# FFN products of the unnormed input, with mean, deviation and bias put in behind them

## The chip, the cores and the metric

The kernel runs on one core of one Trainium2 chip. The metric is the device time of one execution in microseconds (us), as a median of several runs. The engines that matter are PE (TensorE, the matrix unit), DVE (VectorE), ACT (ScalarE), POOL (GpSimd) and SP (SyncE, which here only issues DMAs).

## The reference

One step of a two-layer decoder trunk: layer 0 mixes tokens with RWKV-7, layer 1 with a causal pooling mixer; behind each stands a SwiGLU FFN, and behind every sublayer a layer norm. There are 288 token columns (256 of a prompt, 32 of samples), D = 2048 and a hidden width of 5632, all in fp32.

```python
def _layer_norm(x, g, b):
    mu = jnp.mean(xf, axis=-1, keepdims=True)
    var = jnp.mean(jnp.square(xf - mu), axis=-1, keepdims=True)
    return ((xf - mu) * lax.rsqrt(var + LN_EPS) * g + b)
...
x = _layer_norm(ALPHA * x + mixer(x), ln_g, ln_b)
x = _layer_norm(ALPHA * x + (silu(x @ w_gate) * (x @ w_up)) @ w_down, ln_g, ln_b)
```

## The kernel before

**Layout.** Activations lie transposed: 128 channels on the partitions, 16 chunks of channels (KC), T = 288 token columns in a row. `X` holds the residual, `MH`/`ML` the input of a product, split into a high part in fp32r and the rest.

**One product.** An fp32 product is three fp32r matmuls of 128 x 128 weights with 288 columns (`three`, L723 to L725: high by high, low by high, high by low). Weights come in slabs of 128 x 2048 values for 16 such products. SP issues the DMA of a slab into one of four raw buffers `RAW`; ACT copies its high part to `WH` (`hi`, L1247); DVE subtracts it from the raw one to get `WL` (`lo`, L1677); PE then does the slab's 48 matmuls into one PSUM bank. `WH` and `WL` have two slots, so `hi` of a slab waits until PE has ended the slab two before it. Every engine works through its own instructions in the order in which they are written.

**Start.** The 16 chunks of x are transposed on PE and copied out by ACT and DVE in a loop over c, which also forms r's mixed input (`mix_hi` L1256, `mix_lo` L1692). `first_hi` and `first_lo` put the first two slabs of r between the steps c of that loop. PE waits for all banks of x to be free, then does r's two first columns, alternately by halves of k, then column 2 (`RH`, `RL`), and so on.

**FFN.** Each of the two FFNs has 88 up slabs, alternately of gate and of up, then the down slabs. For a pair of slabs ACT takes the sigmoid of the gate bank (L1552), DVE multiplies it by the gate and the up bank (L2174, L2177), ACT copies the high part `HH` (L1554) and DVE takes the rest `HL` (L2182). In the code of both engines this chain stands behind the `hi` or `lo` of a slab and ahead of the next one's.

**Layer norm ahead of an FFN** (L1522 to L1534 on ACT, L2076 to L2092 on DVE, L1087 and L1094 on PE; norm 0 ahead of FFN 0, norm 2 ahead of FFN 1). A matmul with a constant matrix gives the mean in a bank; DVE centres X in place, four chunks at a time; ACT squares; PE sums the squares over 12 rows (DVE adds the last four rows to the four ahead of them); ACT takes the root and DVE its reciprocal. Then, chunk by chunk, DVE scales by gain and reciprocal, ACT adds the bias once into `MH` and once into X, DVE takes `ML`; PE starts slabs 0 and 1, k by k alternately, as these arrive. A third slab lies split in `W3H`/`W3L`. What stands ahead of norm 0 are the "late" units of the attention's output projection, whose banks DVE adds to X (L2046); ahead of norm 2 it is the pooling mixer (L2295).

```python
for k in range(KC):
    pe.wait_ge(ln["lo"], HALVED[lnk] + k + 1)
    first = up(0, k)
    second = up(1, k)
```

Of the kernel before, what the change touches and what calls it, by code (L numbers as in the profile page):

```python
# [132 lines left out]
def build(nc, x_prompt, x_sample, state_wkv, state_shift, state_pool, ln_g, ln_b, rw_mu, rw_wr, rw_wk, rw_wv,  # L133
# [4 lines left out]
    with ctx:  # L138
# [33 lines left out]
        ML[0] = at("ML0", [P, KC, T], F32R, after("MH0"))  # L172
# [16 lines left out]
        OP = at("OP", [P, KC, T], F32, place["MH1"][0])  # L189

# [158 lines left out]
        hl_ready = sem("hl_ready")  # L349
        act_self = sem("act_self")  # L350
# [121 lines left out]
        ln = {n: sem("ln_" + n) for n in ("x", "mean", "cen", "sq", "var", "sd", "rstd", "scaled", "done", "lo", "sum", "pairs")}  # L472
# [247 lines left out]
        def _(pe):  # L720
# [33 lines left out]
            def first(n, k):  # L754
# [327 lines left out]
            def layer_norm(k):  # L1082
                if k == 2:
                    mean_of(range(13, KC))
                else:
                    pe.wait_ge(ln["x"], KC)
                    pe.matmul(PS[4][:, 0:T], AVG, SUM[:, :], start=True, stop=True).then_inc(ln["mean"], 1)  # L1087
                for q in range(3):
# [29 lines left out]
            def ffn(layer, lnk):  # L1118
                for g in range(2):
# [1239 lines left out]
```

## Time and profile before

| what | us |
|---|---|
| time, median of 3 runs | 2698.59 (2695.88 to 2700.09) |
| time of the profiled execution | 2697.64 |
| span in its trace | 2696.1 |
| PE busy | 2575.9 (96%) |
| DVE busy | 1578.6 (59%) |
| ACT busy | 1131.6 (42%) |
| POOL busy | 142.6 (5%) |

The span runs from the first to the last instruction in the trace; the profiled execution's time has 1.5 us around it. Busy time on PE is that of matmuls which overlap, so it is not PE at its best. In the page's chain of work that ended last, followed back from the end, 82% of the span lie on PE. The DMA engines are busy about half of the time.

### The profile page before, as it was taken

The page shows a single profiled execution, that of the slowest core. Times are in us where ns is not written, and L with a number is a line of the kernel's source. Part 1 is how long each engine was busy: PE and PEld are TensorE (multiplying, and loading weights), DVE is VectorE, ACT ScalarE, POOL GpSimd, SP SyncE. Part 2 cuts the span into 40 slices and gives each one's busy share as a digit, 9 for nine tenths or more (in the row PEclk, how much of TensorE's full clock was granted, in tenths as well). Part 3 has the DMA queues.
Part 4 walks back from the last instruction along what each step waited for, and adds up shares of the span by engine and source line. Part 5 has one row for each costly group of instructions (what it writes and reads, how often), then busy time and mean ns, then how long its engine had stood idle before and what let it go on. Part 6 is the DMA issues. An engine that isn't in the chain of part 4 may idle for free.

```text
span 2696.1 us, 56356 instructions
## 1 busy us (share of the span) xinstructions
PE 2575.9 (96%) x23305; PEld 2476.5 (92%) x23305; DVE 1578.6 (59%) x2400; ACT 1131.6 (42%) x1596; POOL 142.6 (5%) x211
## 2 busy tenths in 40 slices
PE   7989999999999899999999999969999999999997
PEld 7978888888789899999999999958999999999997
DVE  7877888888856644444444444686444444444446
ACT  5565555555533533333333333445333333333334
POOL 0000111111101000000000000100000000000000
PEclk9989999999999899999999999979999999999999
DMA  7622223322336656555665556624555566565553
GB/s 198 197 77 73 80 80 84 84 83 82 92 91 196 156 163 171 160 145 163 187 171 161 165 143 167 175 69 125 166 161 166 145 167 190 160 170 163 142 167 94
DMA packets 707051, 379.33 MB, mean 141 GB/s; under 512 B 16023, under 2 KB 699191, under 8 KB 706711
## 3 DMA queue, kind: packets, MB, share of 16 engines
q1 hardware_dynamic: 701040, 363.46, 48.4%
q0 software_dynamic: 5792, 13.34, 1.9%
q8 instruction: 114, 1.87, 0.3%
q10 hardware_dynamic: 70, 0.39, 0.1%
q14 instruction: 35, 0.29, 0.0%
HBM read 367.31 MB, written 10.62 MB: 140 GB/s over the span
## 4 chain that ended last, share of the span: by engine, by line
PE 82%; DVE 11%; ACT 4%; issue 2%; DMA 1%; POOL 0%; DVEq 0%; ACTq 0%; SPq 0%; POOLq 0%
PE PS L723 25%; PE PS L724 24%; PE PS L725 24%; PE PS L874 2%; DVE WL L1677 2%; ACT WH L1247 1%; DVE PL L1794 1%; DVE ML L1692 1%; PE PS L906 1%; DVE TM L1685 1%; DMA PR<-in_rw_wk 1%; PE PS L993 0%; PE PS L948 0%; PE PS L911 0%; DVE XL L1933 0%
## 5 line engine op out<-in xcount | busy, mean ns | idle before, releaser
L1677 DVE TENSOR_TENSOR WL<-RAW,WH 128x2048 fp32r<-128x2048 f32 (+1 forms) x325 | 658.8, 2027 | 765.6 <-ACT WH L1247 765.6
L723 PE MATMUL PS<-MH,WH 128*128 128x288 f32 (+1 forms) x3152 | 931.2, 295 | 27.0 <-DVE ML L2092 11.3
L724 PE MATMUL PS<-ML,WH 128*128 128x288 f32 (+1 forms) x3152 | 933.7, 296 | 0.0
L725 PE MATMUL PS<-MH,WL 128*128 128x288 f32 (+1 forms) x3152 | 932.7, 296 | 0.0
L1247 ACT ACTIVATE WH<-RAW 128x2048 fp32r<-128x2048 f32 (+1 forms) x325 | 553.6, 1704 | 823.0 <-PE PS L725 808.5
L723 PEld LDWEIGHTS PS<-MH,WH 128*128 128x128 f32 (+1 forms) x3152 | 595.7, 189 | 31.5 <-issue 13.3
L724 PEld LDWEIGHTS PS<-ML,WH 128*128 128x128 f32 (+1 forms) x3152 | 595.7, 189 | 0.2
L725 PEld LDWEIGHTS PS<-MH,WL 128*128 128x128 f32 (+1 forms) x3152 | 595.0, 189 | 0.0
L724 PE MATMUL PS<-HL,WH 128*128 128x288 f32 x1408 | 415.3, 295 | 0.0
L725 PE MATMUL PS<-HH,WL 128*128 128x288 f32 x1408 | 415.0, 295 | 0.0
L723 PE MATMUL PS<-HH,WH 128*128 128x288 f32 x1408 | 413.4, 294 | 0.0
L723 PEld LDWEIGHTS PS<-HH,WH 128*128 128x128 f32 x1408 | 264.7, 188 | 0.1
L724 PEld LDWEIGHTS PS<-HL,WH 128*128 128x128 f32 x1408 | 264.7, 188 | 0.1
L725 PEld LDWEIGHTS PS<-HH,WL 128*128 128x128 f32 x1408 | 264.5, 188 | 0.0
L723 PE MATMUL PS<-MH,PH 128*128 128x288 f32 x768 | 245.0, 319 | 8.4 <-DVE ML L2022 3.8
L724 PE MATMUL PS<-ML,PH 128*128 128x288 f32 x768 | 229.4, 299 | 0.0
L725 PE MATMUL PS<-MH,PL 128*128 128x288 f32 x768 | 228.4, 297 | 0.0
L723 PEld LDWEIGHTS PS<-MH,PH 128*128 128x128 f32 x768 | 146.9, 191 | 33.5 <-issue 22.4
L1554 ACT ACTIVATE HH<-TM 128x288 f32 (+1 forms) x88 | 39.2, 445 | 258.7 <-DVE TM L2177 258.7
L724 PEld LDWEIGHTS PS<-ML,PH 128*128 128x128 f32 x768 | 147.2, 192 | 0.3
L725 PEld LDWEIGHTS PS<-MH,PL 128*128 128x128 f32 x768 | 147.0, 191 | 0.0
L1794 DVE TENSOR_TENSOR PL<-PR,PH 128x512 fp32r<-128x512 f32 x144 | 92.5, 653 | 49.8 <-ACT PH L1348 48.7
(313 smaller groups left out, 2725.1 us busy)
## 6 DMA issues: line engine op xcount, KB each, us to landing
RAW<-in_ffn_w_in SPq DMA_DIRECT2D x176, 1024.0 KB, 5.7
RAW<-in_ffn_w_down SPq DMA_DIRECT2D x128, 704.0 KB, 4.8
RAW<-in_rw_wr SPq DMA_DIRECT2D x16, 1024.0 KB, 6.1
PR<-in_rw_wk SPq DMA_DIRECT2D x64, 256.0 KB, 3.2
PR<-in_rw_wv SPq DMA_DIRECT2D x64, 256.0 KB, 3.1
PR<-in_rw_wo SPq DMA_DIRECT2D x64, 256.0 KB, 3.4
S0N<-in_state_wkv POOLq DMA_DIRECT2D x64, 64.0 KB, 2.3
out<-SOS POOLq DMA_DIRECT2D x64, 64.0 KB, 2.8
```

What stands on the lines that cost most here:

```text
L723: pe.matmul(out, wh, xh, start=first, stop=False)
L724: pe.matmul(out, wh, xl, start=False, stop=False)
L725: return pe.matmul(out, wl, xh, start=False, stop=last)
L874: ins = pe.matmul(bank[hr[r], col + u * CH:col + (u + 1) * CH], lhs(hr[r], u), rhs(hr[r], u), start=True, stop=True)
L906: pe.transpose((PA, PB)[t][:, n * P:(n + 1) * P], f[:, t * P:(t + 1) * P], IDN)
L1247: act.activation(WH[0:rows, j % 2, 0:n], RAW[0:rows, j, 0:n], ACT.Copy).then_inc(hi_ready, 1)
L1554: act.activation(HH[:, bass.ds(hc, 1), :].rearrange("p a t -> p (a t)"), TM[:, b, :], ACT.Copy).then_inc(hh_ready, 1)
L1677: dve.tensor_tensor(WL[0:rows, j % 2, 0:n], RAW[0:rows, j, 0:n], WH[0:rows, j % 2, 0:n].bitcast(F32), ALU.subtract).then_inc(lo_ready, 1)
L1685: dve.scalar_tensor_tensor(out=TM[:, c % 2, :], in0=XX[:, c, :], scalar=PAR[:, row:row + 1], in1=X[:, c, 1:T + 1], op0=ALU.mult, op1=ALU.a ...
L1692: dve.tensor_tensor(ML[m][:, c, :], mixed, MH[m][:, c, :].bitcast(F32), ALU.subtract)\
L1794: dve.tensor_tensor(PL[slot][0:rows, 0:n], PR[slot][0:rows, 0:n], PH[slot][0:rows, 0:n].bitcast(F32), ALU.subtract).then_inc(pc_lo, 1)
```

## The change

The normed input of an FFN is (h - mean) * rstd * g + b. A product with it is rstd * (W (g h) - mean * (W g)) + W b. The changed kernel takes W (g h) with `UH`/`UL`, which hold g h of the unnormed h and behind its 288 columns two more, g and b; so each up matmul has 290 columns, and the bank of a slab gets W g and W b in its columns 288 and 289. The rows of `UH`/`UL` are 1160 bytes long where those of `MH`/`ML` are 1152.

- `UH` (ACT, `input_hi`) and `UL` (DVE, `input_lo`) are formed chunk by chunk in the loop of late units and in the pooling mixer.
- PE does slab 0 whole, with the mean's matmul behind its twelfth k, then slab 1, then the variance (`ln_var`), then the third slab.
- The chain of a pair: ACT copies the two columns of both banks to `C12`; DVE subtracts mean by W g from each bank, multiplies each by rstd; ACT takes the sigmoid with W b as bias; DVE adds W b to the gate and multiplies, the same for the other half; then `HH` and `HL`. That is 7 DVE and 4 ACT instructions where there were 3 and 2.
- The normed X itself, which the residual needs, is formed later: `scaled` (DVE) and `normed` (ACT), a loop of 16 each behind the chain of slabs 2 and 3.
- `lo` of FFN 0's slab 0 stands in the late loop behind the add of unit 12, that of slab 1 behind the loop; both stood behind the norm's centring; `third_lo` stands between centring and the sum of the last four rows.
- r's column 0 goes to bank 6, PE doesn't wait for all of x's banks ahead of it, and the two first slabs are split earlier (`first_hi` behind c = 6 and 11 where it was 10 and 15, `first_lo` behind 8 and 12 where it was 12 and 18).

```diff
+        UH = at("UH", [P, KC, T + 2], F32R, place["MH0"][0] - 128)
+        UL = at("UL", [P, KC, T + 2], F32R, place["ML0"][0] - 128)
...
+        NLN = at("NLN", [P, 2, T], F32, place["LHH"][0] + 4 * T)
+        C12 = at("C12", [P, 2, 4], F32, after("NLN"))
+        GATE = at("GATE", [P, 2, T], F32, after("C12"))
+        LIN = at("LIN", [P, 2, T], F32, after("GATE"))
...
+        def first_bank(n):
+
+            return n % 4 if n else 6
...
-                return three(PS[n % 4][0:wd, 0:T], wh, wl, MH[m][:, k, :], ML[m][:, k, :], k == 0, k == KC - 1)
-
-            pe.wait_ge(x_bank_free, 6 + KC)
+                return three(PS[first_bank(n)][0:wd, 0:T], wh, wl, MH[m][:, k, :], ML[m][:, k, :], k == 0, k == KC - 1)
...
+                if n == 1:
+                    pe.wait_ge(x_bank_free, 6 + KC - 2)
...
+            pe.wait_ge(x_bank_free, 6 + KC)
...
-                        return three(PS[j][:, 0:T], WH[:, j % 2, k * P:(k + 1) * P], WL[:, j % 2, k * P:(k + 1) * P],
-                                     MH[0][:, k, :], ML[0][:, k, :], k == 0, k == KC - 1)
+                        return three(PS[j][:, 0:T + 2], WH[:, j % 2, k * P:(k + 1) * P], WL[:, j % 2, k * P:(k + 1) * P],
+                                     UH[:, k, :], UL[:, k, :], k == 0, k == KC - 1)
...
-                        take_slab(s0 + 1)
-                        take_bank(o0 + 1)
-                        for k in range(KC):
-                            pe.wait_ge(ln["lo"], HALVED[lnk] + k + 1)
-                            first = up(0, k)
-                            second = up(1, k)
-                        first.then_inc(slab_used, 1)
-                        second.then_inc(slab_used, 1)
+                        for j in range(2):
+                            take_slab(s0 + j)
+                            take_bank(o0 + j)
+                            for k in range(KC):
+                                if j == 0:
+                                    pe.wait_ge(ln["lo"], HALVED[lnk] + k + 1)
+                                ins = up(j, k)
+                                if j == 0 and k == KC - 5:
+                                    ln_mean(lnk)
+                            ins.then_inc(slab_used, 1)
+                        ln_var(lnk)
                         third_slab()
...
-                if c in (10, 15):
-                    first_hi(0 if c == 10 else 1)
+                if c in (6, 11):
+                    first_hi(0 if c == 6 else 1)
...
+            def input_hi(k, c):
+
+                act.wait_ge(out_free, 4 + OUT["o" if k == 0 else "pool"] + (c if c < 12 else KC - 1) + 1)
+                act.activation(UH[:, c, 0:T], X[:, c, 1:T + 1], ACT.Copy, scale=par("ln_g", k * KC + c))\
+                   .then_inc(ln["hi"], 1)
...
+            def normed(k):
+
                 with act.Fori(0, KC) as c:
                     act.wait_ge(ln["scaled"], k // 2 * KC + c + 1)
                     xc = X[:, bass.ds(c, 1), 1:T + 1].rearrange("p a t -> p (a t)")
-                    act.activation(MH[0][:, bass.ds(c, 1), :].rearrange("p a t -> p (a t)"), xc, ACT.Identity,
-                                   bias=par("ln_b", k * KC + c))
                     act.activation(xc, xc, ACT.Identity, bias=par("ln_b", k * KC + c)).then_inc(ln["done"], 1)
...
-                                act.activation(TM[:, b, :], PS[j - 1][:, 0:T], ACT.Sigmoid).then_inc(sg_ready, 1)
+                                act.activation(C12[:, b, 0:2], PS[j - 1][:, T:T + 2], ACT.Copy)
+                                act.activation(C12[:, b, 2:4], PS[j][:, T:T + 2], ACT.Copy).then_inc(sums_out, 1)
+                                act.wait_ge(gate_scaled, n + 1)
+                                act.activation(GATE[:, b, :], TM[:, b, :], ACT.Sigmoid, bias=C12[:, b, 1:2])\
+                                   .then_inc(sg_ready, 1)
                                 act.wait_ge(hid_ready, n + 1)
-                                act.activation(HH[:, bass.ds(hc, 1), :].rearrange("p a t -> p (a t)"), TM[:, b, :],
+                                act.activation(HH[:, bass.ds(hc, 1), :].rearrange("p a t -> p (a t)"), LIN[:, b, :],
                                                ACT.Copy).then_inc(hh_ready, 1)
                     if g == 0:
                         up(0, False)
+                        normed(2 * layer)
...
-                if c in (12, 18):
-                    first_lo(0 if c == 12 else 1)
+                if c in (8, 12):
+                    first_lo(0 if c == 8 else 1)
...
+            def input_lo(k, c):
+                dve.wait_ge(ln["hi"], HALVED[k] + c + 1)
+                dve.scalar_tensor_tensor(out=UL[:, c, 0:T], in0=X[:, c, 1:T + 1], scalar=par("ln_g", k * KC + c),
+                                         in1=UH[:, c, 0:T].bitcast(F32), op0=ALU.mult, op1=ALU.subtract)\
+                   .then_inc(ln["lo"], 1)
...
+                            if m == 12:
+                                lo(SLAB["ffn0"], 0)
+                            if 1 <= m <= 12:
+                                dve.wait_ge(ln["hi"], m)
+                                if m == 1:
+                                    gains_lo(0, 0, 12)
...
+            lo(SLAB["ffn0"] + 1, 1)
...
-            def layer_norm(k, beside):
+            def layer_norm(k):
                 n = k // 2
                 dve.wait_ge(ln["mean"], n + 1)
+                dve.wait_ge(ln["lo"], HALVED[k] + KC)
+                dve.tensor_scalar(NLN[:, 0, :], PS[4][:, 0:T], -1.0, None, ALU.mult)
                 for q in range(4):
                     xs = X[:, 4 * q:4 * q + 4, 1:T + 1]
                     dve.tensor_tensor(xs, xs, PS[4][:, 0:T].unsqueeze(1).broadcast_to([P, 4, T]), ALU.subtract)\
                        .then_inc(ln["cen"], 1)
+                third_lo(SLAB["ffn0"] if k == 0 else SLAB["ffn1"])
                 dve.wait_ge(ln["sq"], 4 * n + 4)
                 dve.tensor_tensor(SQ[:, 8:12, :], SQ[:, 8:12, :], SQ[:, 12:16, :], ALU.add).then_inc(ln["pairs"], 1)
-                beside()
                 dve.wait_ge(ln["sd"], 2 * n + 2)
-                dve.reciprocal(LNS[:, 1, :], LNS[:, 0, :]).then_inc(ln["rstd"], 1)
+                dve.reciprocal(NLN[:, 1, :], LNS[:, 0, :]).then_inc(ln["rstd"], 1)
                 dve.wait_ge(ln["rstd"], n + 1)
                 dve.wait_ge(ln["cen"], 4 * n + 4)
 
-                def scaled(c):
+            def scaled(k):
+                with dve.Fori(0, KC) as c:
                     dve.scalar_tensor_tensor(out=xcur(c), in0=xcur(c), scalar=par("ln_g", k * KC + c),
-                                             in1=LNS[:, 1, :], op0=ALU.mult, op1=ALU.mult).then_inc(ln["scaled"], 1)
-                def low(c):
-                    dve.wait_ge(ln["done"], n * KC + c + 1)
-                    dve.tensor_tensor(one(ML[0], c), xcur(c), one(MH[0], c).bitcast(F32), ALU.subtract)\
-                       .then_inc(ln["lo"], 1)
-                for c in range(3):
-                    scaled(c)
-                with dve.Fori(0, KC - 3) as c:
-                    scaled(c + 3)
-                    low(c)
-                for c in range(KC - 3, KC):
-                    low(c)
-                third_lo(SLAB["ffn0"] if k == 0 else SLAB["ffn1"])
+                                             in1=NLN[:, 1, :], op0=ALU.mult, op1=ALU.mult).then_inc(ln["scaled"], 1)
...
+                                gate, lin = TM[:, b, :], LIN[:, b, :]
+                                dve.wait_ge(sums_out, n + 1)
+                                dve.scalar_tensor_tensor(out=gate, in0=NLN[:, 0, :], scalar=C12[:, b, 0:1],
+                                                         in1=PS[j - 1][:, 0:T], op0=ALU.mult, op1=ALU.add)\
+                                   .then_inc(gate_lin, 1)
+                                dve.scalar_tensor_tensor(out=lin, in0=NLN[:, 0, :], scalar=C12[:, b, 2:3],
+                                                         in1=PS[j][:, 0:T], op0=ALU.mult, op1=ALU.add)\
+                                   .then_inc(lin_out, 1)
+                                dve.wait_ge(gate_lin, n + 1)
+                                dve.tensor_tensor(gate, gate, NLN[:, 1, :], ALU.mult).then_inc(gate_scaled, 1)
+                                dve.wait_ge(lin_out, n + 1)
+                                dve.sem_inc(out_free, 2)
+                                dve.tensor_tensor(lin, lin, NLN[:, 1, :], ALU.mult).then_inc(lin_scaled, 1)
                                 dve.wait_ge(sg_ready, n + 1)
-                                dve.tensor_tensor(TM[:, b, :], TM[:, b, :], PS[j - 1][:, 0:T], ALU.mult)\
-                                   .then_inc(hid_self, 1)
-                                dve.wait_ge(hid_self, n + 1)
-                                dve.tensor_tensor(TM[:, b, :], TM[:, b, :], PS[j][:, 0:T], ALU.mult)\
-                                   .then_inc(hid_ready, 1)
-                                dve.wait_ge(hid_ready, n + 1)
-                                dve.sem_inc(out_free, 2)
+                                dve.scalar_tensor_tensor(out=gate, in0=gate, scalar=C12[:, b, 1:2], in1=GATE[:, b, :],
+                                                         op0=ALU.add, op1=ALU.mult).then_inc(gated, 1)
+                                dve.wait_ge(lin_scaled, n + 1)
+                                dve.wait_ge(gated, n + 1)
+                                dve.scalar_tensor_tensor(out=lin, in0=lin, scalar=C12[:, b, 3:4], in1=gate,
+                                                         op0=ALU.add, op1=ALU.mult).then_inc(hid_ready, 1)
                                 dve.wait_ge(hh_ready, n + 1)
-                                dve.tensor_tensor(one(HL, hc), TM[:, b, :], one(HH, hc).bitcast(F32), ALU.subtract)\
+                                dve.tensor_tensor(one(HL, hc), lin, one(HH, hc).bitcast(F32), ALU.subtract)\
                                    .then_inc(hl_ready, 1)
 
                     if g == 0:
                         up(0, False)
+                        scaled(2 * layer)
```

On ACT, at the start of FFN 0, the loop over 16 chunks (L1529 to L1534) stands before ahead of the first `hi` of the loop of slabs:

```order
L1514 ACTIVATE W3H<-RAW 128x2048
L1526 ACTIVATE LNS<-PS 128x288
L1528 ACTIVATE LNS<-LNS 128x288
L1529 UNCONDITIONAL_BRANCH
L1529 ISA
L1532 ISA x2
L1532 ACTIVATE MH_60<-X,PAR 128x288
L1534 ACTIVATE X<-X,PAR 128x288
L1529 REGISTER_ALU
L1529 COMPARE_AND_BRANCH
L1247 ACTIVATE WH<-RAW 128x2048
L1552 ACT_TABLE_LOAD
```

And of the changed kernel, the same engine from the `hi` of slabs 4 and 5 (L1270) to that of slab 6 (the last row):

```order
L1270 ACTIVATE WH<-RAW 128x2048 x2
L1596 ACTIVATE C_88<-PS 128x2
L1597 ACTIVATE C_88<-PS 128x2
L1599 ACTIVATE GATE<-TM,C_88 128x288
L1602 ACTIVATE HH<-LIN 128x288
L1575 UNCONDITIONAL_BRANCH
L1575 ISA
L1578 ISA
L1578 REGISTER_ALU
L1578 ACTIVATE X<-X,PAR 128x288
L1575 REGISTER_ALU
L1575 COMPARE_AND_BRANCH
```

The loop of 16 (L1575 to L1578) has moved from ahead of the first slabs to a place behind the chain of slabs 2 and 3; it has one ACTIVATE in it where there were two, and the `hi` of slab 6 stands right behind it.

On PE, between the last late unit (`PL`) and the first products of the FFN (`WH`), before:

```order
L725 MATMUL PS<-MH_60,PL_83 128x288
L1087 MATMUL PS<-SUM,CP 128x288
L1094 MATMUL PS<-SQ,CP 128x288 x12
L723 MATMUL PS<-MH_60,WH 128x288
L724 MATMUL PS<-ML_61,WH 128x288
```

And after, behind the products of slab 1 (`WL` in the first row), at the third slab (`W3H`):

```order
L742 MATMUL PS<-UL,WH 128x290
L743 MATMUL PS<-UH,WL 128x290
L1116 MATMUL PS<-SQ,CP 128x288 x12
L741 MATMUL PS<-UH,W3H 128x290
L742 MATMUL PS<-UL,W3H 128x290
```

The twelve sums of squares have moved from ahead of slab 0 to behind slab 1, and the products read rows of 290 columns.

## Rows read from the trace of the kernel before

**Rows 1.** The page: busy time by engine, and the chain by engine.

```profile
PE 2575.9 (96%) x23305; PEld 2476.5 (92%) x23305; DVE 1578.6 (59%) x2400; ACT 1131.6 (42%) x1596; POOL 142.6 (5%) x211
...
PE 82%; DVE 11%; ACT 4%; issue 2%; DMA 1%; POOL 0%; DVEq 0%; ACTq 0%; SPq 0%; POOLq 0%
```

**Rows 2.** Stretches: us, PE busy (count), granted clock, DMA share, GB/s.

```profile
950.00:1150.00 200.00, 200.00 (x1515) 1.00 0.60 165
...
902.00:917.00 15.00, 15.00 (x99) 0.87 0.13 34
```

**Rows 3.** Timeline of PE at norm 0: start, us, what, idle before.

```profile
882.70 0.29 PE L725 MATMUL PS<-MH,PL 128*128 128x288 f32 x1
...
892.58 3.56 PE L1094 MATMUL PS<-SQ,CP 128*128 128x288 f32 x14
...
901.88 0.58 PE L723 MATMUL PS<-MH,WH 128*128 128x288 f32 x1 [5.74 <-DVE ML L2092]
902.25 0.44 PE L724 MATMUL PS<-ML,WH 128*128 128x288 f32 x1
902.49 0.44 PE L725 MATMUL PS<-MH,WL 128*128 128x288 f32 x1
...
916.54 0.40 PE L723 MATMUL PS<-MH,W3H 128*128 128x288 f32 x1
```

**Rows 4.** Timeline of PE at the start, r's columns 0 and 2.

```profile
28.69 0.61 PE L723 MATMUL PS<-MH,WH 128*128 128x288 f32 x1 [10.24 <-DVE XPS L1704]
...
43.05 0.29 PE L723 MATMUL PS<-MH,RH 128*128 128x288 f32 x1
```

**Rows 5.** Timeline of DVE at the start: `lo` of r's first two slabs.

```profile
23.84 2.28 DVE L1677 TENSOR_TENSOR WL<-RAW,WH 128x2048 fp32r<-128x2048 f32 x1
...
30.59 2.28 DVE L1677 TENSOR_TENSOR WL<-RAW,WH 128x2048 fp32r<-128x2048 f32 x1
```

**Rows 6.** Timelines of DVE and ACT at norm 0.

```profile
885.20 5.15 DVE L2076 TENSOR_TENSOR X<-X,PS 128x1152 f32<-128x1152 f32 x4 [1.71 <-PE PS L1087]
891.58 1.36 DVE L2079 TENSOR_TENSOR SQ<-SQ 128x1152 f32<-128x1152 f32 x1 [1.23 <-ACT SQ L1522]
...
897.26 1.95 DVE L2082 RECIPROCAL LNS<-LNS 128x288 f32<-128x288 f32 x1
899.24 1.81 DVE L2087 SCALAR_TENSOR_TENSOR X<-X,PAR,LNS 128x288 f32<-128x288 f32 x4
...
918.66 1.28 ACT L1552 ACT_TABLE_LOAD   x1
```

**Rows 7.** Timeline of PE at norm 2: last means, first product, third slab.

```profile
1811.30 2.45 PE L1202 MATMUL PS<-X,CP 128*128 128x288 f32 x8
...
1829.89 0.58 PE L723 MATMUL PS<-MH,WH 128*128 128x288 f32 x1 [5.56 <-DVE ML L2092]
...
1844.72 0.29 PE L723 MATMUL PS<-MH,W3H 128*128 128x288 f32 x1
```

**Rows 8.** A pair of up slabs amid FFN 0: timelines of ACT and DVE.

```profile
1005.75 1.92 ACT L1247 ACTIVATE WH<-RAW 128x2048 fp32r<-128x2048 f32 x1 [4.43 <-PE PS L725]
...
1010.97 0.45 ACT L1554 ACTIVATE HH<-TM 128x288 f32 x1 [3.01 <-DVE TM L2177]
1012.10 1.92 ACT L1247 ACTIVATE WH<-RAW 128x2048 fp32r<-128x2048 f32 x1 [0.68 <-PE PS L725]
...
1009.91 0.45 DVE L2174 TENSOR_TENSOR TM<-TM,PS 128x288 f32<-128x288 f32 x1
...
1014.05 2.29 DVE L1677 TENSOR_TENSOR WL<-RAW,WH 128x2048 fp32r<-128x2048 f32 x1 [2.02 <-ACT WH L1247]
```

**Rows 9.** Two more durations: a DVE instruction that reads a bank; matmuls on unaligned rows.

```profile
L2295 DVE SCALAR_TENSOR_TENSOR X<-PS,PAR,X x16: 507/508/518, 1780.9 to 1811.5; 128x288 f32<-128x288 f32 x16
...
L1202 PE MATMUL PS<-X,CP x32: 403/405/505, 1788.3 to 1813.3; 128*128 128x288 f32 x32
...
L1094 PE MATMUL PS<-SQ,CP x48: 406/406/849, 887.9 to 1823.9; 128*128 128x288 f32 x48
```

More of the change, by code:

```diff
@@ L171, in build @@
         MH[0] = at("MH0", [P, KC, T], F32R, after("LHL"))
-        ML[0] = at("ML0", [P, KC, T], F32R, after("MH0"))
+        ML[0] = at("ML0", [P, KC, T], F32R, after("MH0") + 128)
         MH[1] = at("MH1", [P, KC, T], F32R, after("ML0"))
@@ L189, in build @@
         OP = at("OP", [P, KC, T], F32, place["MH1"][0])
+        UH = at("UH", [P, KC, T + 2], F32R, place["MH0"][0] - 128)
+        UL = at("UL", [P, KC, T + 2], F32R, place["ML0"][0] - 128)
+        assert after("UH") == place["MH0"][1] and after("UL") == place["MH1"][0]
+        NLN = at("NLN", [P, 2, T], F32, place["LHH"][0] + 4 * T)
+        C12 = at("C12", [P, 2, 4], F32, after("NLN"))
+        GATE = at("GATE", [P, 2, T], F32, after("C12"))
+        LIN = at("LIN", [P, 2, T], F32, after("GATE"))
+        assert after("LIN") <= place["UH"][0]
         XROW = at("XROW", [P, 4, 3, 512], F32, place["MH1"][0])
@@ L349, in build @@
         hl_ready = sem("hl_ready")
+        sums_out = sem("sums_out")
+        gate_lin = sem("gate_lin")
+        gate_scaled = sem("gate_scaled")
+        lin_out = sem("lin_out")
+        lin_scaled = sem("lin_scaled")
+        gated = sem("gated")
         act_self = sem("act_self")
@@ L469, in build @@
         OUTPUTS += [("late", m) for m in range(KC)]
-        ln = {n: sem("ln_" + n) for n in ("x", "mean", "cen", "sq", "var", "sd", "rstd", "scaled", "done", "lo", "sum", "pairs")}
+        ln = {n: sem("ln_" + n) for n in ("x", "mean", "cen", "sq", "var", "sd", "rstd", "scaled", "done", "hi", "lo", "sum", "pairs")}
         HALVED = {0: 0, 2: KC}
@@ L1080, in _, with ln_mean @@
                 pass
-            def layer_norm(k):
+            def ln_mean(k):
                 if k == 2:
@@ L1321, in _ @@
                         act.wait_ge(lhl_ready, 4)
-                    act.activation(R[:, c, :], PS[n % 4][:, 0:T], ACT.Copy).then_inc(out_free, 1)
+                    act.activation(R[:, c, :], PS[first_bank(n)][:, 0:T], ACT.Copy).then_inc(out_free, 1)
             hr = [slice(0, HN), slice(HN, P)]
@@ L1482, in _, with gains_hi @@
             act.wait_ge(xkept, 16)
+            def gains_hi(k, a, b):
+                for at, col in ((T, PCOL["ln_g"]), (T + 1, PCOL["ln_b"])):
+                    act.activation(UH[:, a:b, at:at + 1], PAR[:, col + k * KC + a:col + k * KC + b].unsqueeze(2), ACT.Copy)
+            def input_hi(k, c):
+                act.wait_ge(out_free, 4 + OUT["o" if k == 0 else "pool"] + (c if c < 12 else KC - 1) + 1)
+                act.activation(UH[:, c, 0:T], X[:, c, 1:T + 1], ACT.Copy, scale=par("ln_g", k * KC + c))\
+                   .then_inc(ln["hi"], 1)
             def units():
@@ L1498, in units @@
                             act.activation(OP[:, m, :], (D0, D1)[m % 2][:, 0:T], ACT.Copy).then_inc(early_ready, 1)
+                        if kind == "late" and m < 12:
+                            if m == 0:
+                                act.wait_ge(out_free, 4 + OUT["o"] + 1)
+                                gains_hi(0, 0, 12)
+                            input_hi(0, m)
                     yield
@@ L1507, in _ @@
             hi(q, 1, SLAB["ffn0"] + 1)
+            act.wait_ge(out_free, 4 + OUT["o"] + KC)
+            gains_hi(0, 12, KC)
+            for c in range(12, KC):
+                input_hi(0, c)
             def third_hi(s0):
@@ L1656, in _ @@
             pool_alpha(3)
-            pool_slab(4)
+            act.wait_ge(pl["lo"], 4)
+            act.wait_ge(out_free, 4 + OUT["pool"] + 4)
+            gains_hi(2, 0, 4)
+            for c in range(4):
+                input_hi(2, c)
+            pool_slab(4)
+            act.wait_ge(out_free, 4 + OUT["pool"] + 12)
+            gains_hi(2, 4, 12)
+            for c in range(4, 12):
+                input_hi(2, c)
+            act.wait_ge(out_free, 4 + OUT["pool"] + KC)
+            gains_hi(2, 12, KC)
+            for c in range(12, KC):
+                input_hi(2, c)
             pool_slab(5)
@@ L2066, in _ @@
                 pass
+            dve.wait_ge(ln["hi"], 13)
+            gains_lo(0, 12, KC)
+            for c in range(12, KC):
+                input_lo(0, c)
+            lo(SLAB["ffn0"] + 1, 1)
             def xcur(c):
                 return X[:, bass.ds(c, 1), 1:T + 1].rearrange("p a t -> p (a t)")
-            def layer_norm(k, beside):
+            def layer_norm(k):
                 n = k // 2
                 dve.wait_ge(ln["mean"], n + 1)
+                dve.wait_ge(ln["lo"], HALVED[k] + KC)
+                dve.tensor_scalar(NLN[:, 0, :], PS[4][:, 0:T], -1.0, None, ALU.mult)
                 for q in range(4):
@@ L2315, in _, with inputs @@
             outputs(2)
+            def inputs(a, b):
+                dve.wait_ge(ln["hi"], KC + a + 1)
+                gains_lo(2, a, b)
+                for c in range(a, b):
+                    input_lo(2, c)
             lo(SLAB["pool"] + 4, 0)
+            inputs(0, 4)
             outputs(3)
-            def after_pool():
-                lo(SLAB["pool"] + 5, 1)
-            dve.wait_ge(out_free, 4 + OUT["pool"] + KC)
-            layer_norm(2, after_pool)
+            inputs(4, 12)
+            inputs(12, KC)
+            lo(SLAB["pool"] + 5, 1)
+            layer_norm(2)
             dve.wait_ge(tr_stored, 32)
```

17 lines of the change are left out of this document (9 added, 8 removed).

## The prediction

> **What bounds the kernel now.** I read the page's busy times and chain first: PE is busy for 96% of the span, and 82% of the chain that ended last lies on it [rows 1]. So a change pays only where PE stands still or runs slowly, or where it makes PE's own work shorter. The stretch view shows the pace: amid FFN 0, 1515 matmuls in 200 us at full clock, 132.0 ns each [rows 2], so a slab of 48 takes 6.34 us and a pair 12.67. I then looked in the timeline for where PE doesn't keep that pace, at the three places that the change touches.
>
> Norm 0: the last late matmul starts at 882.70 and ends its turn at 882.83; the third slab starts at 916.54 [rows 3]. Between them lie 33.71 us, of which two slabs need 12.67: 21.0 us are lost, to waits, to the squares' sum, and to a start at half clock (matmuls 240 ns apart [rows 3], which is 1.2 GHz; the granted clock is 0.87 over the first 15 us [rows 2], so about 0.13 x 15 = 1.9 us).
>
> Norm 2: from the last means at 1811.30 to the third slab at 1844.72 [rows 7] it is 33.4 us, so 20.7 are lost.
>
> The start: PE begins r at 28.69 after an idle of 10.24, and column 2 at 43.05 [rows 4].
>
> **The change part by part.** The sum is made against the profiled execution, 2697.64 us, of which 2696.1 are the span; the median of the runs is 0.95 above it.
>
> *Wider products.* 88 up slabs in each FFN, of which 88 x 48 = 4224 matmuls, 8448 in both, get two columns more. At full clock a matmul takes 132.0 ns for 288 columns [rows 2], at half clock 240 [rows 3], which is 288 at 1.2 GHz with nothing over, while at 2.4 GHz 288 columns are 120 ns and 12 are over. If the 12 ns are fixed, two columns cost 2/2.4 = 0.83 ns; if all of it goes with the columns, 0.92. That is 7.0 to 7.8 us, and I take 7.3. The lower end is 0: the 12 ns might be a floor that the columns don't reach. The upper end is open, since rows of 1160 bytes are not aligned as those of 1152 are. The nearest rows are the fp32 sums, where X's rows (1156 bytes) take 405 ns and the aligned squares 406 [rows 9]: no price, though these run at half the columns' pace.
>
> The Trainium skill, "TensorE: Matmul & The Clock Gate", section "Back-to-back issue gap", gives N / 2.4 + 2.5 ns between matmuls when warm: 122.5 for 288 columns. The trace has 132.0, so it doesn't agree; by its slope the columns would cost 7.0 us, as by the fixed 12 ns.
>
> *The start.* The order puts `lo` of r's first slab four steps of x earlier and that of the second six. Before, the first stood at 23.84 to 26.12 and the second at 30.59 to 32.87, with 4.5 us of such steps between them [rows 5]; so the second can come some 4.5 earlier at most. The raw data and ACT's copies hold back part of it: I reckon `lo` of the second slab ends at about 29. PE does the first half of column 0 ahead of that, from about 24 (at half clock), and has three halves left, 9.5 us, plus about 0.5 of slow clock: column 2 at 39 to 40, where it was 43.05 [rows 4]. Gain 3.5 us, between 2 and 4.5. What is late next is `lo` of the third column (`RL`), which stands on DVE where it stood, 2.3 us behind the second. Behind it PE is the bound, so the gain stays.
>
> *Norm 0, ahead of the third slab.* PE no longer waits for the norm. What is left of the 21.0 us: the late loop gets `lo` of slab 0 (2.29 [rows 8]) and an instruction of 0.45 per unit on DVE, which delays the last units by 0 to 2.7; I take 1.7, since the loop ends right behind them. The mean's two matmuls at 0.24 each are 0.5. The squares' 24 take 0.242 each (14 span 3.56, of which the last is 0.41 [rows 3]): 5.8, all on PE's path as before. The chain on DVE and ACT that they wait for (minus the mean 0.45, centring 5.15, the last square about as long as a quarter of that, 1.3, `hi` 1.92 and `lo` 2.29 of the third slab, pairs 1.36 [rows 6, 8]: 12.5 from the mean) has beside it the rest of slabs 0 and 1 (four k and one slab, 7.9) and the first 16 of the 24 (3.9), 11.8: a wait of 0.7, taken 0.8. Sum 8.8; gain 12.2, between 10 and 14.
>
> *Norm 0, behind it.* The first pair's chain now waits for the root, the reciprocal (1.95) and a table load (1.28) [rows 6]; the slack of the split ahead covers most of it, I put 0.6 (0 to 1.5). Then the loop of 16. Before, `scaled` and the biases stood on the path of slabs 0 and 1. Now ACT has them between the chain of slabs 2 and 3 and `hi` of slab 6, as the order shows, and DVE between that chain and `lo` of slab 6. `hi` of slab 5 starts when slab 3 ends; with the longer chain (below) `HH` ends 7.7 us later and `HL` at 8.2. Sixteen steps at 0.45 (four in 1.81 [rows 6]) are 7.3, up to 0.53 if a loop's own instructions bound it: ACT ends the last at 15.9 to 17.2. `hi` and `lo` of slab 6 add 1.92 and 2.29: ready at 20.1 to 21.5. PE has slabs 4 and 5 meanwhile, 12.8 with the columns. It stands for 7.3 to 8.7 us, I take 8.0, and then starts at half clock as it did behind the idle stretch at 901.88, +1.8. So 9.8 are given back. Net of norm 0: 12.2 - 0.6 - 9.8 = 1.8 gained.
>
> *Norm 2.* The same. Of 20.7 us remain the last means 2.0, the wait for `lo` of slab 1 behind the pool's last inputs 0.7, the squares 5.8, the wait for the pairs 1.6 (no POOL sum, the mean comes later): 10.1, a gain of 10.6, less 0.6 and 9.8: 0.2.
>
> *The chain of a pair.* No PE work, but it stands ahead of `hi` of the next slab. Before, behind `hi` of the odd slab at 1005.75, `HH` ends at 1011.42, and the next `hi` at 1012.10 waits for PE [rows 8]: 0.7 to spare. Its `lo` ends at 16.34 less 12.10, 4.24 later, and PE needs it 6.34 later: 2.1 more. After: `lo` ends at 4.2, two DVE instructions on banks (0.51 [rows 9]), then gate by rstd, sigmoid, two more on DVE and `HH`, each near the 0.45 of [rows 8] with a semaphore's way between some: 4.2 + 1.0 + 5 x 0.45 + 0.2 = 7.7, where it ended at 5.7. So the next `hi` starts 1.3 late and 2.1 - 1.3 = 0.8 us remain, perhaps 0.5. Free, then; if that cover is gone, each 0.1 us beyond it comes on 86 pairs, 8.6 us.
>
> *The rest* (two gains and biases copied per group, the earlier count of free banks, `UH` and `UL` in the late loop on ACT) lies beside PE's work; SP's order of DMAs is the same.
>
> Sum: +7.3 - 3.5 - 1.8 - 0.2 = +1.8: 2699.4 for the profiled execution, 2700.4 as a median. I give **2700.5**.
>
> **The rivals.** *The columns are free.* Were the 132 ns a floor, as the half clock's exact 240 would allow, the sum falls by 7.3: 2693. Against it: the floor would have to lie at over 121 ns by chance near the columns' own time. The Trainium skill, same page and section, gives pairs of weight load and matmul as 81 ns at N = 128 and 131 at N = 512; on the line between them two columns are 0.26 ns, 2.2 us in all, and the time 2695; but the line has 102 ns at 288 columns, and the trace 132.0.
>
> *The chain overshoots (slower).* If semaphores' ways make the chain over 0.8 us longer than reckoned, the next `hi` comes too late in every pair. It decides from `HH` ending 8.5 us behind the odd `hi`'s start. With 0.1 to 0.2 beyond, 8.6 to 17 us: 2709 to 2718.
>
> *The loop of 16 doesn't stop PE.* If slab 6's parts were ready in time, both 9.8 come back: 2681. The order speaks against it.
>
> *Unaligned rows cost.* 2 ns more per matmul would be 17 us: 2717, and more if they cost more.
>
> **How the numbers follow.** A measurement of this kernel can tell about 0.2%, 5.4 us, from no change: faster is under 2693.2, slower over 2704.0. My forecast has 0.60, with a range of its own of 2695 to 2706 (the two norms' steps are ±3 each): of it 0.03 lie on the faster side and 0.12 on the slower. Free columns 0.14, half of it faster. The overshoot 0.14, all slower. No stop 0.05, faster. Unaligned rows 0.07, slower. In sum: faster 0.15 and a little for errors on that side, 0.18; slower 0.32; same 0.50. The range leaves out the 2681, the larger overshoots and most of the unaligned case: 2691 to 2712.
>
> **What would show it.** Up matmuls 132.8 ns apart amid the FFN (132.0 would be the free columns, 135 the rows); r's column 2 at 39 to 40; the third slab some 21.5 us behind the last late matmul; a PE idle of 7 to 9 us ahead of slab 6 in each FFN, released by DVE's `WL`, and matmuls 240 ns apart behind it; in a pair, `HH` ending 7.7 us behind the odd `hi`'s start, and no idle of PE there. An idle of PE in each pair, or none ahead of slab 6, would make the prediction wrong.

## The result, and the profile after

The changed kernel takes 2719.29 us (median of 4 runs, 2718.26 to 2722.1), the one before 2698.78: ratio 1.0078, 95% interval 1.0066 to 1.0091. It is 20.5 us slower; the forecast was 2700.5, with a range of 2691 to 2712. The profiled execution took 2718.26 us, with a span of 2716.7.

The page of the kernel after, engines, the chain and two groups (busy, mean ns, idle before and its releaser), against [rows 1]:

```profile
PE 2595.1 (96%) x23305; PEld 2494.3 (92%) x23305; DVE 1744.5 (64%) x2764; ACT 1160.1 (43%) x1782; POOL 140.6 (5%) x211
...
PE 80%; DVE 12%; ACT 4%; issue 2%; DMA 1%; DVEq 0%; SPq 0%; ACTq 0%
...
L741 PE MATMUL PS<-UH,WH 128*128 128x290 f32 x2784 | 832.1, 299 | 17.0 <-DVE WL L1739 16.4
...
L741 PE MATMUL PS<-HH,WH 128*128 128x288 f32 x1408 | 413.9, 294 | 3.3 <-DVE WL L1739 3.3
```

PE executes as many matmuls as before and is busy 19 us longer; DVE has 166 us more. Of PE's idles two groups are new: 16.4 us ahead of up products, 3.3 ahead of down products, both released by DVE's `WL`.

The stretch of [rows 2] amid FFN 0, after:

```profile
950.00:1150.00 200.00, 200.00 (x1490) 1.00 0.57 160
```

1490 matmuls where there were 1515, at full clock: 134.2 ns each, 2.2 more than before. (Counts in a stretch come out 0.1 to 0.2 ns below the distance from one start to the next, for every form alike; so the expectations below have 132.2 and 134.4.) Over all up matmuls these are 8448 x 2.2 = 18.6 us, the largest loss that the forecast didn't have: it had 7.3. The loop of 16 costs somewhat more, 20.8 below, but was foreseen.

PE's timeline after, at the places of [rows 3, 4, 7]: r's column 2, the last late unit, the third slab of FFN 0, slab 6, the third slab of FFN 1.

```profile
40.68 0.29 PE L741 MATMUL PS<-MH,RH 128*128 128x288 f32 x1
...
884.43 0.29 PE L743 MATMUL PS<-MH,PL 128*128 128x288 f32 x1
...
904.08 0.51 PE L741 MATMUL PS<-UH,W3H 128*128 128x290 f32 x1
...
938.76 0.60 PE L741 MATMUL PS<-UH,WH 128*128 128x290 f32 x1 [8.20 <-DVE WL L1739]
...
1843.31 0.51 PE L741 MATMUL PS<-UH,W3H 128*128 128x290 f32 x1
```

Where such marks stand after and before gives the account (us; minus is a gain):

| from, to | change | what it holds |
|---|---|---|
| start to r's column 2 | -2.4 | start |
| to the last late matmul | +4.1 | late units +6.3 (most take 1.90 to 2.02 us where it was 1.60, and `lo` of slab 0 stands among them); the stretch ahead of them -2.2 |
| to the third slab of FFN 0 | -14.2 | norm 0 |
| to the first down slab | +15.3 | 42 slabs x 48 x 2.2 ns = 4.5; idle ahead of slab 6, slow clock, first chain: 10.8 together |
| to the third slab of FFN 1 | -4.3 | 44 slabs 4.7, two down phases 1.1 each, norm 2 -11.2 |
| to the end | +22.0 | FFN 1: as above, 15.3 + 4.7 + 2.2 |
| sum | +20.6 | the spans differ by 20.6 |

The late units run from their first add (856.13 before, 851.53 after) to the last late matmul: 26.57 us and 32.90. The stretch ahead of them, from r's column 2, has the same code in both kernels; it took 813.1 us before and 810.9 after, and 812.2 to 815.0 in the profiles of the other variants of the changed kernel. So its -2.2 lie within what executions differ by, and the 6.3 are the price of the late units: in those variants, pool_later below aside, they take 32.6 to 33.2 us.

### The profile page after: what moved, and what is told of

Same layout as the page of the kernel before. It is cut to its first block, busy times and chain, and to the rows that moved or that the text cites. A ratio compares the mean times of both kernels' runs of the same rounds, so it can differ in the third digit from the quotient of the medians.

```text
span 2716.7 us, 56956 instructions
## 1 busy us (share of the span) xinstructions
PE 2595.1 (96%) x23305; PEld 2494.3 (92%) x23305; DVE 1744.5 (64%) x2764; ACT 1160.1 (43%) x1782; POOL 140.6 (5%) x211
## 4 chain that ended last, share of the span: by engine, by line
PE 80%; DVE 12%; ACT 4%; issue 2%; DMA 1%; DVEq 0%; SPq 0%; ACTq 0%
PE PS L741 24%; PE PS L742 23%; PE PS L743 23%; PE PS L894 3%; DVE WL L1739 3%; ACT WH L1270 2%; DVE PL L1856 1%; DVE ML L1754 1%; DVE TM L1747 1%; PE PS L926 1%; PE PS L1013 1%; PE PS L963 0%; PE PS L968 0%; PE PS L931 0%; DVE X L2214 0%
## 5 line engine op out<-in xcount | busy, mean ns | idle before, releaser
L741 PE MATMUL PS<-UH,WH 128*128 128x290 f32 x2784 | 832.1, 299 | 17.0 <-DVE WL L1739 16.4
L1270 ACT ACTIVATE WH<-RAW 128x2048 fp32r<-128x2048 f32 (+1 forms) x325 | 552.0, 1699 | 648.1 <-PE PS L743 644.7
L743 PE MATMUL PS<-UH,WL 128*128 128x290 f32 x2784 | 827.2, 297 | 0.0
L742 PE MATMUL PS<-UL,WH 128*128 128x290 f32 x2784 | 824.7, 296 | 0.0
L741 PEld LDWEIGHTS PS<-UH,WH 128*128 128x128 f32 x2784 | 527.3, 189 | 18.9 <-issue 18.8
L742 PEld LDWEIGHTS PS<-UL,WH 128*128 128x128 f32 x2784 | 530.0, 190 | 0.1
L743 PEld LDWEIGHTS PS<-UH,WL 128*128 128x128 f32 x2784 | 525.7, 189 | 0.0
L1599 ACT ACTIVATE GATE<-TM,C 128x288 f32<-128x288 f32 x88 | 47.2, 537 | 300.3 <-DVE TM L2259 300.3
```

Of the source, the lines that this page charges most:

```text
L741: pe.matmul(out, wh, xh, start=first, stop=False)
L742: pe.matmul(out, wh, xl, start=False, stop=False)
L743: return pe.matmul(out, wl, xh, start=False, stop=last)
L1270: act.activation(WH[0:rows, j % 2, 0:n], RAW[0:rows, j, 0:n], ACT.Copy).then_inc(hi_ready, 1)
L1599: act.activation(GATE[:, b, :], TM[:, b, :], ACT.Sigmoid, bias=C12[:, b, 1:2])\
```

## The experiments

They ask for the price of the columns, of the loop of 16, of the late units, of the down phase's idles and of the start.

### Is it the columns or the rows?

**wide_aligned**, on the kernel before:

```diff
-  three(PS[j][:, 0:T], ..., MH[0][:, k, :], ML[0][:, k, :], ...)
+  three(PS[j][:, 0:n], ..., mh[:, k*T : k*T + n], ml[:, k*T : k*T + n], ...)   # n = T + 2, rows flattened
```

> The kernel before, with 290 columns in the up matmuls of rows k = 0 to 14 of every up slab but the first two of an FFN (the two more columns are the first two of the next row, and their products are left unread); the rows stay 1152 bytes long. So 2 x 86 x 45 = 7740 matmuls are wider. In the changed kernel an up matmul takes 134.4 ns where it took 132.2. Theory A (rows): 0.85 ns of these 2.2 are the two columns, the rest comes from rows of 1160 bytes, which are not aligned. Then the wide matmuls here take about 133.1, +6.6 us: 2705. Theory B (width): any matmul of 290 columns takes 2.2 ns more: +17 us, 2716.

**narrow_unaligned**, on the changed kernel:

```diff
-  three(PS[j][:, 0:T + 2], ..., UH[:, k, :], UL[:, k, :], ...)
+  three(PS[j][:, 0:T], ..., UH[:, k, 0:T], UL[:, k, 0:T], ...)
```

> The changed kernel with 288 columns in its up matmuls, read from the same rows of 1160 bytes; the two columns of gain and bias are not multiplied, and the small copies of their products take two columns of the bank's 288 instead, so the mean's and bias's part is not right. Theory A (rows): the matmuls keep 1.35 of their 2.2 ns, about 133.6 each, and the time falls by 7 us to 2712. Theory B (width): they are back at 132.2 and the time falls by 18.9 us to 2700.

They took 2722.02 us (ratio to the kernel before 1.0083, 1.0066 to 1.0100) and 2713.20 (1.0053, 1.0036 to 1.0070). The stretch from 950 to 1150 us, first of wide_aligned:

```profile
950.00:1150.00 200.00, 200.00 (x1482) 1.00 0.58 162
```

and of narrow_unaligned:

```profile
950.00:1150.00 200.00, 200.00 (x1502) 1.00 0.57 159
```

These are 135.0 ns with 290 columns on aligned rows (135.2 for the wide ones alone, since one k in 16 stayed narrow) and 133.2 with 288 on rows of 1160 bytes, against 132.0. So neither theory holds: both things cost, the width 3.1 ns on aligned rows and the rows 1.1 without the width; together, in the changed kernel, they make 2.2, less than the width alone. (The price of the rows is read from the stretch. The times of narrow_unaligned and the changed kernel differ by 6.1 us and not by 8448 x 1.1 = 9.3, as the stretch ahead of the late units happened to be 4.2 us longer in narrow_unaligned's profile.)

**widths** and **offsets**, on the kernel before, took the two apart, four forms in one kernel each:

```diff
+  cols, at = {(0, 0): (292, 0), (0, 1): (296, 0), (1, 0): (304, 0), (1, 1): (320, 0)}[layer, g]   # widths
+  cols, at = {(0, 0): (288, 2), (0, 1): (288, 8), (1, 0): (288, 16), (1, 1): (290, 8)}[layer, g]  # offsets
+  three(out[:, 0:cols], wh, wl, mh[:, k*T + at : k*T + at + cols], ...)
```

> The kernel before, whose up matmuls of rows k = 0 to 14 (all up slabs but the first two of an FFN) read on into the next row and are 292 columns wide in the first half of FFN 0, 296 in its second half, 304 in the first half of FFN 1 and 320 in its second; rows stay 1152 bytes long, the products of the added columns are left unread. Theory 1 (12 ns fixed and 0.417 ns a column): 133.7, 135.3, 138.7 and 145.3 ns. Theory 2 (a step of about 2 ns beyond 288, then 0.417 a column, as 134.9 at 290 suggests): 135.8, 137.4, 140.8 and 147.4. Theory 3 (the data come in blocks of 16 columns): 292, 296 and 304 take the same, about 139. By theory 1 the time is about 2747, by theory 2 about 2762.

> The kernel before, whose up matmuls of rows k = 0 to 14 (all up slabs but the first two of an FFN) start some columns further on, so that what is multiplied isn't the normed input: 288 columns from 8 bytes on in the first half of FFN 0, from 32 bytes on in its second half, from 64 bytes on in the first half of FFN 1, and 290 columns from 32 bytes on in its second half. Rows stay 1152 bytes apart. Theory (a row's start that is no multiple of 64 bytes costs by itself): about 133.2, as 288 columns on rows of 1160 bytes took, then 133 or less, then 132.2 again, and 135 for the 290. Rival (the row's length between rows matters, not its start): 132.2 in the first three.

A stretch of each half of an FFN, widths:

```profile
955.00:1175.00 220.00, 220.00 (x1627) 1.00 0.58 159
1360.00:1580.00 220.00, 220.00 (x1627) 1.00 0.58 161
1920.00:2100.00 180.00, 180.00 (x1302) 1.00 0.57 158
2360.00:2540.00 180.00, 180.00 (x1242) 1.00 0.54 151
```

and offsets:

```profile
955.00:1175.00 220.00, 220.00 (x1646) 1.00 0.58 160
1360.00:1580.00 220.00, 220.00 (x1664) 1.00 0.59 164
1920.00:2100.00 180.00, 180.00 (x1355) 1.00 0.59 162
2360.00:2540.00 180.00, 180.00 (x1332) 1.00 0.56 156
```

Length by count, with the narrow k taken out, gives for the wide ones 135.4 ns at 292 columns, 135.4 at 296, 138.7 at 304, 145.8 at 320. Theory 1 has 135.3, 138.7 and 145.3 for the last three: 12 ns and 0.417 a column. But 290 (135.2) and 292 cost what 296 does. So on these rows a price by blocks of 8 columns, 32 bytes, fits all four: the two columns are paid as eight, 8 / 2.4 = 3.3 ns. Nothing between 296 and 304 columns was run, and the runs don't tell whether the block lies in what PE reads or in what it writes to the bank. Theory 3 (blocks of 16) falls with 296 against 304, theory 2 (one step, then by the column) with 290, 292 and 296 alike. From offsets: 288 columns that start 8 bytes off cost 133.8, 32 bytes off 132.2, 64 bytes off 132.9, and 290 at 32 bytes 135.3. The rival there (132.2 in the first three) falls with the 133.8: the start itself has a price. A start inside a block costs, one at a block's edge 32 bytes off doesn't, which fits; that the first costs 1.8 and not a whole block, that 64 bytes off costs 0.9, and that 290 columns on rows of 1160 bytes (134.2) are cheaper than on aligned ones, doesn't. So that the two columns and their rows cost 2.2 ns is measured; why it is 2.2 is open. The two took 2752.49 and 2709.65 us, one execution each.

### Is it the loop of 16 that stops PE?

**norm_later**, on the changed kernel (ACT; DVE's `scaled` likewise):

```diff
     if g == 0:
         up(0, False)
-        normed(2 * layer)
...
             hi(s1 // 4 + i + (j + 2) // 4, (j + 2) % 4, s1 + 4 * i + j + 2, HH2 * P)
+            if g == 0 and j % 2 == 0:
+                normed(2 * layer, 2 * i + j // 2)
```

> The changed kernel, with the loop of 16 (normed X) taken from behind the chain of slabs 2 and 3 and put, one chunk at a time, behind the split of every second down slab of the first half, ahead of the add that needs it. Theory: the idle of PE ahead of slab 6, 8.5 us in each FFN, and the slow clock behind it, 1.8, go, and nothing takes their place, since a down slab has a shorter chain: -20 us, 2699. Rival: the added 0.45 us of both engines per two down slabs hold back the next split, as the chain of the last pair does (PE idles 1.13 us at each start of a down phase): half or more of it comes back, 2708 or more.

2700.62 us (1.0006, 0.9997 to 1.0016): 18.7 less than the changed kernel, near the theory's 20. From the third slab to the first down slab PE takes 271.5 us in both FFNs, where the changed kernel takes 282.1 and 281.8: the loop costs 10.5 and 10.3, 20.8 in all. The idle of PE ahead of up products, 17.0 us in the page above, falls to 0.6, and the idle ahead of down products hasn't grown (3.4 us, where it was 3.3), so the rival falls:

```profile
L741 PE MATMUL PS<-UH,WH 128*128 128x290 f32 x2784 | 829.9, 298 | 0.6 <-DVE X L2386 0.2
```

In the changed kernel, ACT's timeline ahead of slab 6:

```profile
924.67 0.44 ACT L1602 ACTIVATE HH<-LIN 128x288 fp32r<-128x288 f32 x1 [1.21 <-DVE LIN L2268]
926.29 8.22 ACT L1578 ACTIVATE X<-X,PAR  x16 [1.17 <-DVE X L2178]
934.42 3.69 ACT L1270 ACTIVATE WH<-RAW 128x2048 fp32r<-128x2048 f32 x2
```

The `hi` of slab 6 starts when the sixteenth step ends, 8.2 us after the loop's first.

### What do the late units wait for?

**late_order**, on the changed kernel (ACT):

```diff
-  if kind == "late" and m < 12:
+  if kind == "late" and 1 <= m <= 12:
...
-      input_hi(0, m)
+      input_hi(0, m - 1)
```

> The changed kernel, with ACT's high part of g h taken one late unit later, so that it stands behind the split of a coming weight slab and no longer waits for the add of its own unit ahead of it. In the changed kernel the late units come every 1.95 us, in the one before every 1.6. Theory: this chain (add, high part, split of the weights on ACT, its rest on DVE, next add) sets the 1.95; the units come every 1.6 again and about 4 us are won, 2715. Rival: DVE's added work per unit sets it, and the units stay at 1.9 or more: 2718 to 2719.

2721.23 us (1.0081, 1.0065 to 1.0098): nothing was won, the units still come every 1.90 to 2.02 us, and the theory fell. The timelines of DVE and POOL in the changed kernel, one unit:

```profile
868.82 0.44 DVE L2121 TENSOR_TENSOR X<-X,PS 128x288 f32<-128x288 f32 x1
869.18 0.51 DVE L2089 SCALAR_TENSOR_TENSOR UL<-X,PAR,UH 128x288 fp32r<-128x288 f32 x1
869.61 1.29 DVE L1844 TENSOR_TENSOR PL<-PR,PH 128x512 fp32r<-128x512 f32 x1
...
869.34 1.02 POOL L708 TENSOR_TENSOR SUM<-SUM,X 128x288 f32<-128x288 f32 x1 [1.00 <-DVE X L2121]
```

`PL` took 0.68 before and takes 1.29 here; it ends 0.54 us behind POOL's sum, as if most of it were done only then. POOL's sum in turn ends 0.67 us behind `UL`, and alone it takes 0.69. Before, `PL` stood right behind the add and was ahead of POOL, so that POOL waited, which cost nothing:

```profile
869.01 0.68 DVE L1782 TENSOR_TENSOR PL<-PR,PH 128x512 fp32r<-128x512 f32 x1
...
869.17 1.19 POOL L690 TENSOR_TENSOR SUM<-SUM,X 128x288 f32<-128x288 f32 x1 [0.52 <-DVE X L2046]
```

**pl_first** (DVE) puts it back there:

```diff
-          input_lo(0, m - 1)
   unit_lo(e + AHEAD)
+  if late and 1 <= m <= 12:
+      input_lo(0, m - 1)
```

> The changed kernel, with DVE's low part of g h in the late units behind the split of the coming weights (PL) where it stood ahead of it. In the changed kernel PL takes 1.18 to 1.30 us where it took 0.68, and it ends 0.55 us behind POOL's sum, which starts when the add of the unit ends; before, PL stood right behind the add and began ahead of POOL. Theory: PL waits for POOL's instruction, and the units come every 1.6 us again: -4 us, 2715. Rival: the low part meets the same wait, or DVE's added 0.43 us set the pace: 2718 or 2719.

2718.13 us (1.0065, 1.0050 to 1.0081), within 1.2 of the changed kernel, and the late units take 32.65 us where they took 32.90. The rival was right: DVE's timeline shows the same wait on the other instruction.

```profile
870.54 0.68 DVE L1844 TENSOR_TENSOR PL<-PR,PH 128x512 fp32r<-128x512 f32 x1
871.14 1.06 DVE L2089 SCALAR_TENSOR_TENSOR UL<-X,PAR,UH 128x288 fp32r<-128x288 f32 x1
872.13 0.44 DVE L2121 TENSOR_TENSOR X<-X,PS 128x288 f32<-128x288 f32 x1
```

**pool_later** takes POOL away from the units:

```diff
-  pool.wait_ge(ready, at + c + 1)
+  pool.wait_ge(ready, at + KC)
```

> The changed kernel, in which POOL's 16 sums for the mean of norm 0 wait for the last late unit, so that POOL does nothing beside the late units. Theory (POOL's sum and DVE's instructions on two tensors of SBUF exclude each other, and the two, 0.7 + 0.6 + 0.43 us and the add of 0.37, set the 1.95 us): the units come every 1.6 us again, PL takes 0.68 and the low part 0.51. Rival (DVE's added instruction sets the pace by itself): they stay at 1.8 to 1.95. The mean comes about 8 us later than in the changed kernel, since 16 sums of 0.7 stand behind the last add, so the whole gets slower in either case: by the theory 2723, by the rival 2727.

```profile
869.32 0.46 DVE L2121 TENSOR_TENSOR X<-X,PS 128x288 f32<-128x288 f32 x1
869.69 0.51 DVE L2089 SCALAR_TENSOR_TENSOR UL<-X,PAR,UH 128x288 fp32r<-128x288 f32 x1
870.12 0.69 DVE L1844 TENSOR_TENSOR PL<-PR,PH 128x512 fp32r<-128x512 f32 x1
870.92 0.46 DVE L2121 TENSOR_TENSOR X<-X,PS 128x288 f32<-128x288 f32 x1
```

The adds are 1.60 us apart again, and neither instruction is drawn out. The late units take 28.23 us (853.45 to 881.68): of the 6.3 by which they had grown, 4.7 go with POOL, and 1.7 stay for DVE's added work. So POOL's sum it is, together with DVE's added instruction. (The whole, in one execution, took 2729.93 us, more than the theory's 2723: the mean comes later, and 15 of POOL's sums then took 15.4 us, not the 0.7 each that was reckoned.) The Trainium skill says it on "SBUF — State Buffer", section "SBUF: two separate sides": of a DVE instruction with two inputs in SBUF and a GpSimd instruction that reads SBUF, the one that starts first holds their shared port for its whole length, and the other waits. The trace agrees: `PL` and `UL`, with two such inputs, are drawn out. The add takes one input from PSUM; in the kernel before, where one at 867.04 falls into three POOL sums in a row (865.15 to 868.65), it takes 0.46, while the `PL` ahead of it at 865.95 takes 0.93.

### The start alone, and a joined kernel

**start_only** is the kernel before with the change's start:

```diff
-  if c in (10, 15):   # first_hi
+  if c in (6, 11):
...
-  if c in (12, 18):   # first_lo
+  if c in (8, 12):
...
+  def first_bank(n): return n % 4 if n else 6
```

> The kernel before with the change's start alone: r's column 0 in bank 6, the waits for x's banks behind it, and the first two slabs split behind c = 6 and 11 and behind 8 and 12. Theory: r's column 2 begins 2.5 us earlier, as it does in the changed kernel, PE is the bound behind it, and the whole is won: 2696.4. Rival: the gain is lost on the way to FFN 0, where PE waits for other engines or for DMAs: 2698 to 2699.

2696.28 us against 2698.29 (0.9991, 0.9982 to 1.0000): about 2.0 won, though the interval just reaches no change. r's column 2 begins at 40.69, 2.4 earlier than in [rows 4], so little is lost on the way.

**joined** has norm_later, pl_first and, on ACT in the chain of a half's last pair:

```diff
   act.activation(GATE[:, b, :], TM[:, b, :], ACT.Sigmoid, ...)
+  if last and j == 3:
+      hi((s0 + 2 * HG) // 4, 2, s0 + 2 * HG + 2, HH2 * P)
   act.wait_ge(hid_ready, n + 1)
```

> The changed kernel with three edits: the normed X chunk by chunk in the down phase (2700.6 by itself), DVE's low part of g h behind PL, and, in the chain of the last pair of each half, ACT's high part of the third down slab ahead of HH. The theory of the down phase: the four idles of 1.13 us there come from that high part, which stands behind the longer chain. By the theories 4 us go for the late units and 3 to 4 for these idles: 2692 to 2693. Rivals: one of the two gives nothing, 2696 to 2697; or the wait at a down phase's start moves to HL, and only the late units' part is seen.

2695.61 us against 2698.93 (0.9986, 0.9977 to 0.9995): it beats both kernels, by 3.3 and by 23.7, but misses the 2692 to 2693 that were expected. PE's down group in it has no idle left, where the changed kernel had 3.3 us:

```profile
L741 PE MATMUL PS<-HH,WH 128*128 128x288 f32 x1408 | 413.9, 294 | 0.0
```

Against norm_later it is 5.0 less. Its four down phases are 0.9 us shorter each than norm_later's, 3.6 in all, so the edit of the last pair gives what was expected. The 4 us for the late units didn't come, as pl_first had shown by then: they take 32.60 us, where norm_later has 33.20. Of the 3.3 won against the kernel before, the start alone gives 2.0; what the unnormed input brings even in this form is the rest, 1.3, which is not clear of noise.

## Why the prediction was wrong, step by step

- **Wider products: the step that failed.** I put two columns at 0.83 to 0.92 ns, as if the price went by the column, and the rows at nothing. It was 2.2 ns, 18.6 us and not 7.3; 11.3 of the 18.8 us by which the forecast was off. The runs showed 3.1 ns for two columns on aligned rows, which fits a price by blocks of 8 columns, and 1.1 ns for rows of 1160 bytes by themselves; why the two together make 2.2 is open. My bound for the rows, X's fp32 sums [rows 9], didn't carry over; they run at half the columns' pace, as I had noted. The rival on unaligned rows named 2 ns more and 2717, at a chance of 0.07. That it came close is luck: its 2 ns come on top of the columns' 0.87, it lays them on the rows alone, and it has nothing for the late units and the down phases. The Trainium skill, "TensorE: Matmul & The Clock Gate", section "Back-to-back issue gap", has N / 2.4 + 2.5 ns, and so 0.417 ns a column, for an isolated matmul, not for the stream that the prediction set it against; the trace of this stream agrees on the step from 296 to 320 columns (0.41 to 0.44) and not for two single ones.
- **The start.** 3.5 forecast, 2.4 measured at column 2 (40.68, where 39 to 40 was named): inside the 2 to 4.5, somewhat high.
- **Late units.** 1.7 forecast, 2.7 at most; they cost 6.3, of which the marks show 4.1 only because the stretch ahead of them was 2.2 shorter. The 1.7 was right for DVE's added work, as far as pool_later's one execution shows. I had looked at DVE and ACT and not at POOL, whose sums stand beside every unit and make the other 4.7. The wait could be read before the change: POOL's sum takes 1.19 us beside `PL` there and 0.69 without it.
- **Norm 0.** From the last late matmul to the third slab I had two slabs and 7.1 us; it is 19.65, less two slabs of 6.44, thus 6.8: right. (The 21.5 named as a sign had the late units' 1.7 in it, which come ahead of this mark.) **Norm 2:** gain of 10.6 forecast, 11.2 measured: right.
- **The loop of 16.** An idle of 8.0 and 1.8 of slow clock forecast; 8.2 idle, and the granted clock 0.50, the lower level, over the 4.4 us behind it, 0.84 over 15 us. Together 10.5 and 10.3 by norm_later, where 9.8 was forecast: right. The rival without a stop is out.
- **The chain of a pair.** `HH` was to end 7.7 us behind the odd `hi`. The changed kernel's ACT timeline, against [rows 8]:

```profile
1005.64 1.92 ACT L1270 ACTIVATE WH<-RAW 128x2048 fp32r<-128x2048 f32 x1 [3.32 <-PE PS L743]
...
1012.98 0.45 ACT L1602 ACTIVATE HH<-LIN 128x288 f32 x1 [1.31 <-DVE LIN L2268]
1013.50 1.92 ACT L1270 ACTIVATE WH<-RAW 128x2048 fp32r<-128x2048 f32 x1
```

  It ends at 1013.43, 7.8 behind, and PE has no idle there: right, with the cover of half a us. What I missed is the last pair of a half: a down slab has 33 matmuls, so the cover is 2 us shorter there, and each of the four down phases grew by 1.1 us, 4.4 in all (0.83 of each is idle in the page; the 1.13 of two expectations is from one start to the next). The forecast had this at nothing.

Put right, the sum is 18.2 (86 slabs of each FFN; the first two stand in the norms' marks) - 2.4 + 4.1 - 14.2 - 11.2 + 21.6 (idle, slow clock and first chain of both FFNs) + 4.4 = 20.5, of 20.6 measured. It closes since its terms are read from the marks of the same two profiles; the experiments are what ties them to their causes.

## What to carry to other kernels

Before columns are added to a matmul that fills a PE-bound loop, measure one stretch with them: two columns can cost more than twice the price by the column, 8448 times. Work that is moved off the critical path needs a place with slack on its own engines, also in the last turn of a loop, where the following phase is shorter. And ask, before the change, of each added DVE instruction on two tensors in SBUF what POOL does at that time.

## What the runs showed of the hardware that I had not expected

fp32r matmuls of 290, 292 and 296 columns take the same 135.2 to 135.4 ns on aligned rows (132.0 at 288, 138.7 at 304). Rows of 1160 bytes cost 288 columns 1.1 ns, yet take 0.9 off the price of 290; why is open. POOL's 0.7 us sum draws out a DVE instruction with two inputs in SBUF from 0.68 to 1.29 us, and which one is only a matter of order; one with an input in PSUM stays at 0.46.
